# Where the weight tiles and the activations of a two-block transformer kernel begin in SBUF

## The chip, the cores and the metric

The kernel runs on one core of a Trainium2 chip. The metric is the device time in microseconds (us) of one launch. Tensors in SBUF are given here by the byte at which they begin within a partition; what this text calls the residue of a tensor is that byte modulo 512.

## What is computed

Two transformer blocks with 256 tokens and a model width of 1024, all in float32. The first block has two layers with a second stream of 256 context tokens; the second has one layer. Cut to what matters here:

```python
def swiglu(h, w_gu, w_down):
    gu = h @ w_gu
    return (jax.nn.silu(gu[..., :D_FF]) * gu[..., D_FF:]) @ w_down
...
    for i in range(DEPTH):            # first block, streams x and z (context)
        x = ffn_sublayer(x, mx, 0, g[0], g[1], ffn_w_gu[i, 0], ffn_w_down[i, 0])
        if ctx_needed:
            z = ffn_sublayer(z, mz, 0, g[0], g[1], ffn_w_gu[i, 0], ffn_w_down[i, 0])
        ...                           # window attention (i = 1) or short convolution (i = 0)
        x = ffn_sublayer(x, mx, 6, g[4], g[5], ffn_w_gu[i, 1], ffn_w_down[i, 1])
...
    for i in range(DEPTH_2):          # second block: two sparse attentions, gates, one swiglu
        proj = rms_norm(x, g_mix[i]) @ w_in[i]
        ...
        x = x + merged @ w_out[i]
        gate, up = jnp.split(rms_norm(x, g_ffn[i]) @ w_ffn_in[i], 2, axis=-1)
        x = x + (jax.nn.silu(gate) * up) @ w_ffn_out[i]
        ple_gate = jax.nn.sigmoid(rms_norm(x, g_ple[i]) @ w_ple_gate[i])
        x = x + ple_gate * (p[i] @ w_ple_proj[i])
```

## The kernel before

The weights stream through SBUF in units of up to 128 x 2048 float32 (1 MB), one after another in a fixed list, `UNITS`. A unit belongs to a phase such as `gu0b` (gate and up weights, second part, of feed-forward 0) or `dn0bx` (down weights, stream x). Each unit has two buffers of each of three kinds, taken by the unit's parity: the SyncE queue loads `w_raw`, ScalarE rounds it into `w_hi` (float32r, L1539), VectorE writes the remainder `w_raw - w_hi` into `w_lo` (L944). The activations are split in the same way into a high and a low tensor: `h0`/`h1` and `hid0`/`hid1` in the first block, `b2_h0`/`b2_h1`, `b2_h3_0`/`b2_h3_1` and `b2_hid0`/`b2_hid1` in the second. A product is then the sum of three float32r matmuls (`PARTS`): high weights with high activations, high with low, low with high. `feature_unit` (L560) issues them: for each 128 x 128 weight tile `k`, the weights are the stationary operand and 256 or 512 columns of the activations the moving one. Every matmul has its own weight load; PEld is TensorE's weight load in the profile. `gu3` moves 258 columns. `token_unit` (L574) has the roles exchanged: weights move, activations stand.

Two streams of 256 tokens lie beside each other in `h` and `hid`. Phases whose inputs are ready for both streams move 512 columns (`gu0a`, `dn0a`, `gu0b`, the same of feed-forwards 1 and 2, and `conv_b`); all others move 256. In the trace the tensors `b2_h` and `b2_h3` are both called `b_h`, `b2_hid` is called `b_hid`.

The tensors of SBUF lie one behind another in the order in which `build` allocates them, so each size moves all that follow. Some residues come from tensors that are only there to fill, such as `skip2`. Worked out from the order and the sizes:

| operand of TensorE | residue before | residue after |
|---|---|---|
| `w_hi`, `w_lo`, phases with 512 columns but `conv_b` | 192 | 192 |
| `w_hi`, `w_lo`, all other phases and `conv_b` | 192 | 0 |
| `h0`, `h1`, `b2_h`, `b2_h3` | 256 | 192 |
| `hid0`, `hid1` | 288 | 192 |
| `b2_hid`, `p_r` | 384 | 192 |
| `x`, `gate_tmp`, `prod`, `sq`, `ssum` | 192 | 128 |
| `y` | 0 | 448 |
| `mats` (identity, mean, swaps) | 192 | 192 |

All weight tiles within a unit are 512 or 1024 bytes apart, and the activation tiles 1024 or 2048, so the residue is the same for each matmul of a phase.

What orders the work around this: TensorE waits in `feature_unit` for `lo_made` (the half unit is split) and for `evac` of the unit two before. ScalarE's queue is written out by hand: behind the evacuation of unit u comes the second half of unit u+2 (`high_half(u + 2, 1)`) and then the first half of unit u+3 (`high_ahead`). The first half may begin when TensorE has done the first half of the unit that had the buffer before (`half_done`); the second half waits for `unit_done`. Where a unit is larger than the one before in its buffer (`grows`) the first half waits for `unit_done` too.

Of the kernel before, what the change touches and what calls it, by code (L numbers as in the profile page):

```python
# [134 lines left out]

def halves_by(tile, *names):

    return max(HALVED[u] + 1 for u in phase_units(*[n for n in names if n in FIRST]) if UNITS[u].ul == tile)


def grows(u):

    return UNITS[u].elems > UNITS[u - 2].elems or UNITS[u - 2].phase == "ple_proj"

# [9 lines left out]
def build(nc, t, out, vec_at):  # L154
# [3 lines left out]
    def sb(name, shape, dt=F32, stack=None):  # L158
        return (stack or mem).enter_context(nc.sbuf_tensor(name, list(shape), dt))
# [11 lines left out]
    w_hi = [sb(f"w_hi{j}", [P, UNIT], F32R) for j in range(2)]  # L171
    w_lo = [sb(f"w_lo{j}", [P, UNIT], F32R) for j in range(2)]
# [30 lines left out]
    apart.close()  # L203
    hid1 = [sb(f"hid{j}", [P, HID, T2], F32R, b1) for j in range(2)]
# [7 lines left out]
    sb("skip2", [P, 2, S], F32, b2)  # L212
# [4 lines left out]
    causal = sb("causal", [P, S + 30], F32, b2)  # L217
    p_r = [sb(f"p_r{j}", [P, 2, S], F32R, b2) for j in range(2)]
# [11 lines left out]
    hid2 = [sb(f"b2_hid{j}", [P, HID, S], F32R, b2) for j in range(2)]  # L230

# [270 lines left out]
    def tensor_program():  # L502
# [41 lines left out]
        def feature_unit(u, acts, kc, mt, ready=None, beside=None, one_bank=False):  # L544
            w = [w_[u % 2][:, 0:kc * mt * P].rearrange("p (k n) -> p k n", k=kc) for w_ in (w_hi, w_lo)]
# [19 lines left out]
        def token_unit(u, acts, beside=None):  # L565
            w = [w_[u % 2][:].rearrange("p (k n) -> p k n", k=NC) for w_ in (w_hi, w_lo)]
# [286 lines left out]
        def up_phase():  # L853
            for u in phase_units("w_up"):
                w = [w_[u % 2][:].rearrange("p (k n) -> p k n", k=NC) for w_ in (w_hi, w_lo)]
# [14 lines left out]
        def ple():  # L870
            u = FIRST["ple_proj"]
            w = [w_[u % 2][:].rearrange("p (k n) -> p k n", k=2) for w_ in (w_hi, w_lo)]
# [33 lines left out]
    def vector_program():  # L906
# [32 lines left out]
        def low_half(u, n):  # L939
            if u < len(UNITS):  # L940
                half = UNITS[u].elems // 2
                cols = slice(n * half, (n + 1) * half)
                dve.wait_ge(hi_made, 2 * u + n + 1)
                dve.tensor_tensor(w_lo[u % 2][:, cols], w_raw[u % 2][:, cols], w_hi[u % 2][:, cols].bitcast(F32),  # L944
                                  ALU.subtract).then_inc(lo_made, 1)
# [584 lines left out]
    def scalar_program():  # L1530
        def high_half(u, n):
            if u < len(UNITS):
# [4 lines left out]
                if u >= 2:  # L1537
                    act.wait_ge(half_done if n == 0 and not grows(u) else unit_done, u - 1)
                act.activation(w_hi[u % 2][:, cols], w_raw[u % 2][:, cols], ACT.Copy).then_inc(hi_made, 1)  # L1539
# [679 lines left out]
```

## Time and profile before

| | |
|---|---|
| median of 3 runs | 2189.11 us (2188.25 to 2189.54) |
| time of the profiled execution | 2193.29 us |
| span of the profiled execution | 2191.9 us |
| TensorE busy | 2117.4 us, 97% |
| VectorE busy | 1532.0 us, 70% |
| ScalarE busy | 1046.2 us, 48% |
| HBM read | 375.45 MB, 172 GB/s over the span |
| mean granted TensorE clock | 0.991 |

The profiled execution is 4.18 us longer than the median. The duration of a matmul in the profile is from its start to its modelled end and overlaps with the next one; what a stream of matmuls costs is the pitch, the time from one start to the next. Where a stretch is filled with matmuls of one kind, the pitch is (length of the stretch + duration of one) / (number of matmuls that touch it), since the number counts those in flight at both ends. A windows row gives the stretch and its length, then for each engine (PE, PEld, and where all are shown DVE, ACT, POOL) the busy time and in brackets the number of instructions, then the granted clock as a share of 2.4 GHz, the DMA share and the rate in GB/s.

### The profile page before, as it was taken

Reading aid. Unit: us, or ns where it says so; the run is one execution under the profiler, and the core shown is the slowest. Engines: PE = TensorE matmul, PEld = TensorE weight load, DVE = VectorE, ACT = ScalarE, POOL = GpSimd, SP = SyncE. Lnnn points to the kernel's source line nnn. Section 1 sums busy time; section 2 is a strip of 40 time slices with the busy share of each in tenths; the row PEclk is TensorE's granted clock in tenths of the full one; section 3 lists DMA queues with packets and bytes.
Section 4 is the critical chain, followed back from the end, with each engine's and each line's share of the span. In section 5 each row is a group of like instructions: output and inputs, shape, how many; then the busy total and the mean of one; then the engine's idle time right before and its main releaser. Section 6 shows DMA issues by size and latency. Waiting matters only on the chain. (4 is left out here: it accounts for less than half of the span.)

```text
span 2191.9 us, 35166 instructions
## 1 busy us (share of the span) xinstructions
PE 2117.4 (97%) x14546; PEld 1914.2 (87%) x14546; DVE 1532.0 (70%) x2435; ACT 1046.2 (48%) x1675; POOL 91.6 (4%) x67
## 2 busy tenths in 40 slices
PE   6999999999999999999999999998999799999998
PEld 4988889998899888899988899868999787799998
DVE  3665777887785667787566777876665677777665
ACT  5622224763584232367323236675444445655444
POOL 1000000100100000010000001001000001000000
PEclk9999999999999999999999999999999899999999
DMA  7545555555445455555555555403555541245554
GB/s 308 200 162 203 190 182 182 173 177 191 171 173 184 169 202 191 173 184 184 174 181 195 192 173 177 166 7 129 171 196 187 202 147 67 81 175 171 202 178 143
DMA packets 70014, 378.76 MB, mean 173 GB/s; under 512 B 7392, under 2 KB 12384, under 8 KB 42976
## 3 DMA queue, kind: packets, MB, share of 16 engines
q1 hardware_dynamic: 66960, 369.92, 48.0%
q10 hardware_dynamic: 2896, 6.60, 0.8%
q8 instruction: 115, 1.88, 0.3%
q14 instruction: 43, 0.35, 0.0%
HBM read 375.45 MB, written 1.05 MB: 172 GB/s over the span
## 5 line engine op out<-in xcount | busy, mean ns | idle before, releaser
L560 PE MATMUL ps_g<-h,w_hi 128*128 128x256 f32 (+2 forms) x4288 | 983.6, 324 | 14.0 <-DVE h L1049 8.0
L944 DVE TENSOR_TENSOR w_lo<-w_raw,w_hi 128x1024 fp32r<-128x1024 f32 (+2 forms) x614 | 690.7, 1128 | 337.6 <-ACT w_hi L1539 336.0
L1539 ACT ACTIVATE w_hi<-w_raw 128x1024 fp32r<-128x1024 f32 (+2 forms) x614 | 591.2, 968 | 548.0 <-PE ps_g L560 381.9
L560 PEld LDWEIGHTS ps_g<-h,w_hi 128*128 128x128 f32 x4288 | 716.0, 189 | 82.6 <-issue 15.8
L560 PE MATMUL ps_g<-h,w_lo 128*128 128x256 f32 (+2 forms) x2144 | 688.9, 321 | 0.0
L560 PE MATMUL ps_g<-hid,w_hi 128*128 128x256 f32 (+1 forms) x2368 | 494.8, 306 | 1.9 <-DVE hid L1247 0.9
L560 PEld LDWEIGHTS ps_g<-h,w_lo 128*128 128x128 f32 x2144 | 404.8, 189 | 33.7
L560 PEld LDWEIGHTS ps_g<-hid,w_hi 128*128 128x128 f32 x2368 | 383.5, 189 | 25.8 <-DVE w_lo L944 1.4
L560 PE MATMUL ps_g<-hid,w_lo 128*128 128x256 f32 (+1 forms) x1184 | 361.2, 305 | 0.0
L560 PE MATMUL ps_g<-b_h,w_hi 128*128 128x256 f32 x1504 | 276.5, 285 | 10.2 <-DVE b_h L1049 7.2
L560 PEld LDWEIGHTS ps_g<-b_h,w_hi 128*128 128x128 f32 x1504 | 232.1, 190 | 18.0 <-issue 16.9
L560 PEld LDWEIGHTS ps_g<-hid,w_lo 128*128 128x128 f32 x1184 | 222.2, 188 | 11.0
L560 PE MATMUL ps_g<-b_h,w_lo 128*128 128x256 f32 x752 | 211.4, 281 | 0.0
L909 DVE CUSTOM_DVE_ANT_0 ps_s<-mod_raw,cond_b,vecs 128x1024 f32<-128x1024 f32 x128 | 164.9, 1288 | 15.6 <-DMA mod_raw<-in_w_mod 15.6
L909 DVE CUSTOM_DVE_ANT_0 mod_raw<-mod_raw,cond_b,vecs 128x1024 f32<-128x1024 f32 x128 | 169.3, 1322 | 0.0
L1686 ACT ACTIVATE gate_tmp<-ps_g 128x256 f32<-128x256 f32 (+1 forms) x102 | 48.7, 478 | 247.0 <-PE ps_g L560 246.9
L2004 POOL TENSOR_TENSOR ssum<-ssum,sq 128x512 f32<-128x512 f32 x56 | 81.0, 1446 | 1972.4 <-ACT sq L1564 1972.4
L1098 DVE TENSOR_TENSOR prod<-gate_tmp,ps_g 128x512 f32<-128x512 f32 (+1 forms) x86 | 48.3, 562 | 135.1 <-ACT gate_tmp L1686 135.1
L560 PEld LDWEIGHTS ps_g<-b_h,w_lo 128*128 128x128 f32 x752 | 142.7, 190 | 0.0
L560 PE MATMUL ps_g<-b_hid,w_hi 128*128 128x256 f32 x352 | 60.4, 277 | 2.8 <-DVE w_lo L944 1.4
L1139 DVE TENSOR_TENSOR hid<-prod,hid 128x256 fp32r<-128x256 f32 (+1 forms) x108 | 57.5, 532 | 0.0
L1737 ACT ACTIVATE hid<-prod 128x256 fp32r<-128x256 f32 (+1 forms) x108 | 54.0, 500 | 6.2 <-DVE prod L1098 5.1
(274 smaller groups left out, 1592.8 us busy)
## 6 DMA issues: line engine op xcount, KB each, us to landing
w_raw<-in_gu SPq DMA_DIRECT2D x130, 1024.0 KB, 4.8
mod_raw<-in_w_mod SPq DMA_DIRECT2D x128, 512.0 KB, 3.5
w_raw<-in_conv_cu SPq DMA_DIRECT2D x16, 1024.0 KB, 4.8
w_raw<-in_dn00b SPq DMA_DIRECT2D x16, 768.0 KB, 4.2
w_raw<-in_dn01b SPq DMA_DIRECT2D x16, 768.0 KB, 4.2
w_raw<-in_dn10b SPq DMA_DIRECT2D x16, 768.0 KB, 4.2
w_raw<-in_conv_out SPq DMA_DIRECT2D x8, 1024.0 KB, 4.8
w_raw<-in_w_in_a SPq DMA_DIRECT2D x8, 1024.0 KB, 5.4
```

The source lines that it names most:

```text
L560: mm = pe.matmul(at, w[wp][:, k, m * P:(m + 1) * P], acts[ap][:, k, cs], start=(k == 0 and n == 0 and not (one_bank and m)), stop=(k == kc ...
L909: return dve.tensor_tensor_reduce(into, w, cond_b[:, s, :], 1.0, b_mod[:, g, s:s + 1], ALU.mult, ALU.add, mod_sb[:, g, s:s + 1])
L944: dve.tensor_tensor(w_lo[u % 2][:, cols], w_raw[u % 2][:, cols], w_hi[u % 2][:, cols].bitcast(F32), ALU.subtract).then_inc(lo_made, 1)
L1098: dve.tensor_tensor(prod[:, j, cs], gate_tmp[:, j, cs], ps_g[:, 2 * j + 1, cs], ALU.mult).then_inc(evac, 1)
L1139: dve.tensor_tensor(hid[1][:, ul, cs], prod[:, j, cs], hid[0][:, ul, cs].bitcast(F32), ALU.subtract).then_inc(half_lo, 1)
L1539: act.activation(w_hi[u % 2][:, cols], w_raw[u % 2][:, cols], ACT.Copy).then_inc(hi_made, 1)
L1686: act.activation(gate_tmp[:, j, cs], ps_g[:, 2 * j, cs], ACT.Silu if ph[:2] == "gu" else ACT.Copy).then_inc(gate_made, 1)
L1737: act.activation(hid[0][:, ul, cs], prod[:, j, cs], ACT.Copy).then_inc(half_hi, 1)
L2004: pool.tensor_tensor(ssum[:, s, :], ssum[:, s, :], sq[:, s, :], ALU.add).then_inc(sq_added[s], 1)
```

## The change

Weight tiles get two places in their buffers. Phases that move 512 columns (except `conv_b`) have them at one place, all others 80 elements (320 bytes) further, modulo 128 elements. The two starts of each buffer (`HI_STARTS`, `LO_STARTS`) make up for where the buffer itself lies, so that high and low tiles of both parities have one residue. The buffers are longer by 80 or 96 elements, and `fill0`, `fill1` and `fill2` (with `skip2` taken away) put `h`, `hid`, `b2_h`, `b2_hid` and `p_r` all at residue 192. The operands of ScalarE's and VectorE's split and of all of TensorE's units follow. No instruction is added, removed or moved in order, and no shape changes.

Where a unit begins further up in a buffer than the unit before it did, ScalarE's write of its first half would run into weights that TensorE has yet to read; there the wait is for `unit_done` instead of `half_done` (`moves_up`). By the list of units that holds for 12 of them: the first two units of `gu0a`, `dn0bx`, `gu1a`, `dn1bx`, `gu2a` and `dn2bx`.

```diff
+def weight_slot(u):
+    return 0 if UNITS[u].cols == BOTH and UNITS[u].phase != "conv_b" else 80
+
+HI_STARTS, LO_STARTS = (0, 80), (48, 0)
+
+def weight_at(u, starts):
+    return (weight_slot(u) - starts[u % 2]) % P
...
+def moves_up(u):
+    return any(weight_at(u, starts) > weight_at(u - 2, starts) for starts in (HI_STARTS, LO_STARTS))
...
-    w_hi = [sb(f"w_hi{j}", [P, UNIT], F32R) for j in range(2)]
-    w_lo = [sb(f"w_lo{j}", [P, UNIT], F32R) for j in range(2)]
+    w_hi = [sb(f"w_hi{j}", [P, UNIT + (80, 96)[j]], F32R) for j in range(2)]
+    w_lo = [sb(f"w_lo{j}", [P, UNIT + 80], F32R) for j in range(2)]
+    sb("fill0", [P, 32])
...
+    sb("fill1", [P, 120], F32, b1)
     hid1 = [sb(f"hid{j}", [P, HID, T2], F32R, b1) for j in range(2)]
...
-    sb("skip2", [P, 2, S], F32, b2)
...
+    sb("fill2", [P, 96], F32, b2)
     p_r = [sb(f"p_r{j}", [P, 2, S], F32R, b2) for j in range(2)]
...
+    def hi_of(u):
+        at = weight_at(u, HI_STARTS)
+        return w_hi[u % 2][:, at:at + UNIT]
...
-            w = [w_[u % 2][:, 0:kc * mt * P].rearrange("p (k n) -> p k n", k=kc) for w_ in (w_hi, w_lo)]
+            w = [w_[:, 0:kc * mt * P].rearrange("p (k n) -> p k n", k=kc) for w_ in (hi_of(u), lo_of(u))]
...
-                dve.tensor_tensor(w_lo[u % 2][:, cols], w_raw[u % 2][:, cols], w_hi[u % 2][:, cols].bitcast(F32),
+                dve.tensor_tensor(lo_of(u)[:, cols], w_raw[u % 2][:, cols], hi_of(u)[:, cols].bitcast(F32),
...
-                    act.wait_ge(half_done if n == 0 and not grows(u) else unit_done, u - 1)
-                act.activation(w_hi[u % 2][:, cols], w_raw[u % 2][:, cols], ACT.Copy).then_inc(hi_made, 1)
+                    act.wait_ge(unit_done if n or grows(u) or moves_up(u) else half_done, u - 1)
+                act.activation(hi_of(u)[:, cols], w_raw[u % 2][:, cols], ACT.Copy).then_inc(hi_made, 1)
```

## Rows read from the trace of the kernel before

**Rows 1.** The page: busy time of each engine, and TensorE's granted clock in slices
```profile
PE 2117.4 (97%) x14546; PEld 1914.2 (87%) x14546; DVE 1532.0 (70%) x2435; ACT 1046.2 (48%) x1675; POOL 91.6 (4%) x67
...
PEclk9999999999999999999999999999999899999999
```

**Rows 2.** Lines by form: L560's groups, count, busy us, mean ns, idle before
```profile
L560 PE MATMUL ps_g<-h,w_hi 128*128 128x512 f32 x1600 | 498.4, 393 | 0.0
L560 PE MATMUL ps_g<-h,w_hi 128*128 128x256 f32 x1984 | 357.9, 282 | 5.9 <-DVE h L1041 2.9 <-DVE prod L1098 1.5 <-DVE w_lo L944 1.3
L560 PE MATMUL ps_g<-hid,w_hi 128*128 128x256 f32 x1888 | 343.5, 283 | 1.9 <-DVE hid L1247 0.9 <-DVE y L1116 0.8
...
L560 PE MATMUL ps_g<-b_h,w_hi 128*128 128x256 f32 x1504 | 276.5, 285 | 10.2 <-DVE b_h L1049 7.2 <-DVE qk L1346 2.6 <-DVE b_h L1442 0.4
...
L560 PE MATMUL ps_g<-hid,w_hi 128*128 128x512 f32 x480 | 151.3, 396 | 0.0
L560 PE MATMUL ps_g<-h,w_hi 128*128 128x258 f32 x704 | 127.5, 284 | 8.0 <-DVE h L1049 8.0
...
L560 PE MATMUL ps_g<-b_hid,w_hi 128*128 128x256 f32 x352 | 60.4, 277 | 2.8 <-DVE w_lo L944 1.4 <-DVE x L1116 1.4
```

**Rows 3.** Windows of L560: stretch, length, PE busy (count), PEld busy (count), clock, DMA, GB/s
```profile
470.00:510.00 40.00, 40.00 (x342) 40.00 (x341) 1.00 0.57 194
344.00:374.00 30.00, 30.00 (x253) 30.00 (x252) 1.00 0.66 228
1600.00:1666.00 66.00, 66.00 (x559) 66.00 (x558) 1.00 0.52 185
2055.00:2120.00 65.00, 65.00 (x554) 65.00 (x553) 1.00 0.55 189
2027.00:2052.00 25.00, 25.00 (x223) 25.00 (x223) 1.00 0.63 209
215.00:340.00 125.00, 125.00 (x548) 102.57 (x547) 1.00 0.54 187
157.00:208.00 51.00, 51.00 (x220) 41.05 (x219) 1.00 0.50 180
```

**Rows 4.** Timeline of w_up (L865): start us, busy us, instruction, count
```profile
1920.99 0.39 PE L865 MATMUL ps_g<-b_hid,w_hi 128*128 128x256 f32 x2
...
1921.34 0.39 PE L865 MATMUL ps_g<-b_hid,w_hi 128*128 128x256 f32 x2
...
1921.67 0.39 PE L865 MATMUL ps_g<-b_hid,w_hi 128*128 128x256 f32 x2
```

**Rows 5.** Windows of L865: w_up while the clock is 1.2 GHz, and after
```profile
1922.20:1925.20 3.00, 3.00 (x16) 3.00 (x15) 0.50 0.84 289
...
1928.00:1944.00 16.00, 16.00 (x138) 16.00 (x137) 1.00 0.43 138
```

**Rows 6.** Line L574, two token units: duration ns min/median/max, first and last start
```profile
L574 PE MATMUL ps_g<-w_hi,b_h x32: 281/281/384, 1796.2 to 1801.7; 128*128 128x256 f32 x32
...
L574 PE MATMUL ps_g<-w_hi,b_h x32: 276/276/366, 1805.4 to 1810.7; 128*128 128x256 f32 x32
```

**Rows 7.** Windows, all engines: conv_cux, conv_outx, w_in_d, dn4b
```profile
416.00:466.00 50.00, 49.28 (x403) 48.72 (x404) 42.52 (x57) 36.28 (x62) 3.44 (x2) 1.00 0.48 169
555.00:578.50 23.50, 23.42 (x196) 23.21 (x195) 21.93 (x27) 12.61 (x16) 3.20 (x2) 1.00 0.51 184
1817.00:1918.00 101.00, 98.06 (x777) 75.69 (x776) 75.76 (x299) 58.21 (x184) 5.54 (x4) 0.98 0.21 75
2120.70:2157.20 36.50, 33.66 (x290) 32.92 (x288) 22.08 (x32) 17.21 (x26) 2.94 (x2) 1.00 0.46 154
```

**Rows 8.** The chain of waits within dn4b: start us, us, what
```profile
2122.58 0.97 DVE w_lo L944
...
2123.57 4.18 DMA w_raw<-in_dn2b
...
2141.69 1.62 DVE w_lo L944
```

**Rows 9.** Timeline of ScalarE where gu0b (512 columns) gives way to dn0bx (256)
```profile
341.31 0.60 ACT L1686 ACTIVATE gate_tmp<-ps_g 128x512 f32<-128x512 f32 x1 [4.59 <-PE ps_g L560]
341.81 0.84 ACT L1539 ACTIVATE w_hi<-w_raw 128x768 fp32r<-128x768 f32 x1
```

More of the change, by code:

```diff
@@ L230, in build, with lo_of @@
     hid2 = [sb(f"b2_hid{j}", [P, HID, S], F32R, b2) for j in range(2)]
+    def hi_of(u):
+        at = weight_at(u, HI_STARTS)
+        return w_hi[u % 2][:, at:at + UNIT]
+    def lo_of(u):
+        at = weight_at(u, LO_STARTS)
+        return w_lo[u % 2][:, at:at + UNIT]
     b_mod = vecs[:, vec_at["b_mod"]:vec_at["b_mod"] + 2 * N_MODS].rearrange("p (m s) -> p m s", s=2)
@@ L565, in token_unit @@
         def token_unit(u, acts, beside=None):
-            w = [w_[u % 2][:].rearrange("p (k n) -> p k n", k=NC) for w_ in (w_hi, w_lo)]
+            w = [w_.rearrange("p (k n) -> p k n", k=NC) for w_ in (hi_of(u), lo_of(u))]
             pe.wait_ge(lo_made, 2 * u + 2)
@@ L854, in up_phase @@
             for u in phase_units("w_up"):
-                w = [w_[u % 2][:].rearrange("p (k n) -> p k n", k=NC) for w_ in (w_hi, w_lo)]
+                w = [w_.rearrange("p (k n) -> p k n", k=NC) for w_ in (hi_of(u), lo_of(u))]
                 for src in range(2):
@@ L871, in ple @@
             u = FIRST["ple_proj"]
-            w = [w_[u % 2][:].rearrange("p (k n) -> p k n", k=2) for w_ in (w_hi, w_lo)]
+            w = [w_.rearrange("p (k n) -> p k n", k=2) for w_ in (hi_of(u), lo_of(u))]
             pe.wait_ge(p_lo, 1)
```

## The prediction, made before the changed kernel ran

> **What bounds the kernel now.** I read the page first: TensorE is busy 97% of the span, the next engine 70%, and the clock is full in nearly every slice [rows 1]. So TensorE's stream sets the time. Then the lines by form, for what the stream consists of: nearly all of it is L560 in a few forms [rows 2]. The counts there are those with `w_hi`; by `PARTS` each form has half as many again with `w_lo`. With 256 columns that makes 2976 matmuls on `h`, 2832 on `hid`, 2256 on `b_h`, 528 on `b_hid`; 1056 on `h` with 258 columns; with 512 columns 2400 on `h` and 720 on `hid`. The idle time before them is 29 us in these rows, little against 2190.
>
> Then windows that lie inside one phase and are filled with L560, since the pitch is what counts [rows 3]. Pitch = (length + duration of one) / count, with durations of 0.28 us (0.39 at 512 columns) from [rows 2]:
> - conv_cuz (470 to 510), `h`, 256 columns: 40.28/342 = 117.8 ns
> - dn0bx (344 to 374), `hid`: 30.28/253 = 119.7
> - gu3b (1600 to 1666), `h`, 258 columns: 66.28/559 = 118.6
> - gu4b (2055 to 2120), `b_h`: 65.28/554 = 117.8
> - dn4a (2027 to 2052), `b_hid`: 25.28/223 = 113.4
> - gu0b (215 to 340), `h`, 512 columns: 125.39/548 = 228.8
> - dn0a (157 to 208), `hid`, 512 columns: 51.39/220 = 233.6
>
> The reader should see that one shape, 128x256, has three pitches, and they go with the residue of the moving tensor: with weights at 192, activations at 256 give 117.8, at 288 give 119.7, at 384 give 113.4. DVE and ACT do nothing to these stretches, PE is busy in all of each. At 512 columns 288 is again slower than 256, by 4.8 ns. PEld is busy all the time at 256 columns and 80% at 512: the load of the next weights always runs beside a moving stream. The distance from activation to weight residue is thus a cost, and the change sets it: to 192 bytes (192 minus 0, as dn4's 384 minus 192) in phases of 256, to 0 in those of 512.
>
> **Against this speaks the Trainium skill.** "TensorE: Matmul & The Clock Gate", Part 2, says that TensorE has two independent SBUF read ports and that loading the next tile's weights takes nothing from the running matmul. By that rule the placement changes nothing; it is a rival below. The rows of dn4a and gu4b contradict it, by 4.4 ns a matmul in one shape [rows 3]. The same page's gap formula, N/2.4 + 2.5 ns, would put an undisturbed matmul at an estimated 109 ns for 256 columns and 216 for 512.
>
> **Term 1, 256 columns.** dn4a is the one row with the new distance, so 113.4 is what I take. `h`: 2976 x (117.8 - 113.4) = 13.1 us. `b_h`: 2256 x 4.4 = 9.9. 258 columns: 113.4 x 258/256 = 114.3, 1056 x 4.3 = 4.5. `hid`: 2832 x 6.3 = 17.8. `b_hid`: nothing. Together 45.3; the mean clock of 0.991 means about 2% of the span at 1.2 GHz, where [rows 5] show 3.41/16 = 213 ns, which is 256 columns at 1.2 GHz with nothing on top, so nothing to save: 44.5 us. That residues count as a distance and not each by itself is an assumption: no row has weights at 0.
>
> **Term 2, the long pitch.** One distance can have two pitches. w_up has dn4's residues. It runs three matmuls in 0.33 to 0.35 us, 113 ns each, before the clock drops [rows 4], and after the clock is back 16.28/138 = 118.0, to its end [rows 5]. Two token units with the same operands' residues (weights now moving) show 281 ns of duration in one and 276 in the next [rows 6]; 276 is dn4's. So the stream can lock into a long pitch of 118 or a short one of 113, and a drop of the clock or a pause may decide which. dn4 itself went into the short one. I take a quarter of the 9120 matmuls to be caught: 2280 x 4.4 = 10 us lost. The ends are 0 and all of them.
>
> **Term 3, 512 columns, distance 0.** No row has it. At distance 96 the pitch is 233.6, at 64 it is 228.8; a line through the two gives 219.2 at 0. The other end is 228.8, no further gain. I take 222, nearer to the line, since the same step from 96 to 64 also helps at 256 columns. `conv_b` (192 of the 2400) gets distance 192 with 512 columns, which no row shows, and is left at 228.8, plus or minus 1 us. Sum: 2208 x 6.8 + 720 x 11.6 = 15.0 + 8.4 = 23.4 us; ends 3.5 (only `hid` gains) and 2208 x 9.6 + 720 x 14.4 = 31.6.
>
> **Term 4, what doesn't reach the end.** A faster stream shortens the cover of other engines. VectorE is busy 85% in conv_cux and 93% in conv_outx, 75% in w_in_d with two attentions' chains [rows 7]: of the 960 matmuls there, 4 us of saving may be lost. Down phases have the shortest units: at 113 ns a unit of 36 takes 4.1 us, and a load of its weights takes 4.18 from issue to landing, with a split behind it [rows 8]. dn4b runs at that pitch and has 33.66 us of work in 36.50 [rows 7], so up to 2.8 us is lost in each of seven such phases that now run at 119.7, if their saving of 1.8 each allows; I take 3 us over all.
>
> The new wait (`moves_up`) delays ScalarE's first half for 12 units. Behind it in ScalarE's queue stands the evacuation of the unit that TensorE has just finished, whose VectorE product and `hid` tile dn0bx needs. In [rows 9] that evacuation comes at 341.31, at once when the unit is done; the first half, 0.85 us long by the row behind it, now stands ahead of it. dn0bx needs the last `hid` tile only after 33 of its matmuls, 3.7 us, and that hides most: 0 to 0.8 us at three places, I take 1. Before gu0a the next unit is 11 us off (48 x 228.8 ns), which hides it all. The fp32 matmuls (mean, transposes) get other distances too; no row prices them, and I take 0 within plus or minus 1.5 us. Term 4: 8 us.
>
> **Sum.** 44.5 + 23.4 - 10 - 8 = 49.9 us off 2193.3, the profiled execution's time: 2143.4. The median of the runs is 4.2 below that: 2139.
>
> **The rivals.**
> 1. The long pitch holds at 256 columns almost everywhere. For it: w_up stays at it for the rest of its phase, and few places reset the stream, since residues no longer change between w_up and the end. Against it: dn4 was entered from a 117.8 stream. `hid` gains 2832 x 1.9 = 5.4, dn4 loses 528 x 4.4 = 2.3, 512 columns give 23.4, less 4 for cover: 22 us, 2167.
> 2. As 1, and distance 0 does nothing at 512 columns: 5.4 - 2.3 + 3.5 = 7 us, 2183.
> 3. Nothing moves, by the skill's rule of independent ports, or because the residues count each by itself and weights at 0 are no better than `h` at 256: 2189, with 512 columns unchanged.
> 4. Slower: at distance 0 both streams start in the same place of SBUF and collide on every matmul. The trend from 96 to 64 speaks against it, but 0 lies outside the two rows. `hid` already shows what a worse distance does, 4.8 ns. If 512 columns take 238, that is 2208 x 9.2 + 720 x 4.4 = 23.5 us more; with rival 1's 3.1 of gain the kernel is 20 us slower, 2209. It decides from 231 ns at 512 columns, if the long pitch holds too; with term 1 whole it would need 243.
>
> **How the numbers follow.** Forecast 2139 with chance 0.65 (its own range 2117 to 2162: terms 1 and 3 whole with term 4 halved give 44.5 + 31.6 - 4 = 72 off, and half the matmuls at the long pitch with term 3 at 10 give some 27); rival 1 0.20; rival 2 0.05; rival 3 0.05; rival 4 0.05. The range 2110 to 2173 leaves out the last three and the edges. About 0.2% is what a measurement of this kernel can tell from no change. Faster: 0.65 + 0.20 + 0.05 = 0.90; same 0.05; slower 0.05.
>
> **What would show it.** In windows of the same phases: 113.4 at `h`, `hid` and `b_h` (duration 276) shows term 1, 118 with 281 the long pitch; gu0b and dn0a at one pitch near 222 shows term 3, one at or above 229 refutes it; both should be equal, since they have one distance. `conv_b` apart from gu0a shows whether 0 was needed. Gaps in front of dn0bx's last tiles and in conv_outx price term 4. I am wrong if a phase with weights at 0 and activations at 192 differs from dn4a before, without a drop of the clock ahead of it.

## The result, and the profile after

| | before | after |
|---|---|---|
| median | 2189.11 us | 2177.78 us |
| lowest to highest, 7 runs each | 2183.54 to 2190.56 | 2172.7 to 2182.31 |
| profiled execution, its span | 2193.29, 2191.9 | 2176.27, 2174.7 |

The ratio is 0.9947, with a 95% interval of 0.9935 to 0.9959. The change makes the kernel 0.5% faster, where 2.3% was forecast, and the time lies above the forecast's range of 2110 to 2173.

In this text a distance is the residue of the weight tiles minus that of the activations, modulo 512. Before, the distances were 448 (`h`, `b_h`), 416 (`hid`) and 320 (`b_hid`). After the change there are two: 0 in phases with 512 columns, 320 in all others and in `conv_b`. The prediction counted from the other side, so its 64, 96 and 192 are 448, 416 and 320 here.

The page of after, busy time by engine and the granted clock; the answer to [rows 1]:

```profile
PE 2091.3 (96%) x14546; PEld 1892.2 (87%) x14546; DVE 1529.4 (70%) x2435; ACT 1043.1 (48%) x1675; POOL 90.8 (4%) x67
...
PEclk9999999999999999999999999999999999999999
```

TensorE's busy share fell from 97% to 96%: besides a faster stream there is more idle time. The lines by form, with mean duration and idle time before the group, answer [rows 2] (L560 is now L588, L944 is L972, L1116 is L1144, L1539 is L1567):

```profile
L588 PE MATMUL ps_g<-h,w_hi 128*128 128x512 f32 x1600 | 493.2, 390 | 0.0
L588 PE MATMUL ps_g<-h,w_hi 128*128 128x256 f32 x1984 | 353.1, 282 | 7.5 <-DVE h L1069 3.8 <-DVE prod L1126 2.2 <-DVE w_lo L972 1.1
L588 PE MATMUL ps_g<-hid,w_hi 128*128 128x256 f32 x1888 | 331.6, 280 | 7.1 <-DVE y L1144 4.5 <-DVE hid L1275 0.9 <-DVE w_lo L972 0.6
...
L588 PE MATMUL ps_g<-h,w_hi 128*128 128x258 f32 x704 | 130.2, 287 | 7.5 <-DVE h L1077 7.5
```

Two things stand out. The form with 258 columns got slower, 284 to 287 ns. And before `hid` there is a wait for `y`, VectorE's addition of a finished down unit to the result, of 4.5 us, which was 0.8.

Windows of TensorE inside single phases answer [rows 3]. In order: conv_cuz, gu1az, dn0bx, gu3b, gu4b, dn4a, dn3a, gu0b, dn0a, conv_b. Columns: stretch, length, busy (count), clock, DMA share, GB/s:

```profile
468.00:508.00 40.00, 40.00 (x342) 1.00 0.56 197
660.00:690.00 30.00, 30.00 (x257) 1.00 0.56 199
344.00:373.00 29.00, 28.57 (x241) 1.00 0.63 224
1600.00:1656.00 56.00, 56.00 (x465) 1.00 0.52 179
2042.00:2102.00 60.00, 60.00 (x532) 1.00 0.55 195
2014.00:2038.00 24.00, 24.00 (x214) 1.00 0.64 223
1565.00:1588.00 23.00, 23.00 (x197) 1.00 0.65 227
222.00:336.00 114.00, 114.00 (x505) 1.00 0.54 187
158.00:206.00 48.00, 48.00 (x214) 1.00 0.52 188
512.00:552.00 40.00, 40.00 (x173) 1.00 0.56 197
```

Taken as before, (length + duration) / count, with 0.28 and 0.39 us: conv_cuz 117.8, gu1az 117.8, dn3a 118.2, but gu4b 113.3 and dn4a 113.5, all with 256 columns at one distance. gu3b is at 121.0, which was 118.6. gu0b is at 226.5 and dn0a at 226.1 (one matmul more or less in the count is 1 ns there), conv_b at 233.5. dn0bx has gaps.

From the starts of all matmuls in the two traces, each pitch added up by kind, and what goes beyond a pitch counted as a pause:

| part | before, us | after, us | change | mean pitch, ns |
|---|---|---|---|---|
| 256 columns, `h` | 350.5 | 346.4 | -4.1 | 117.8 to 116.4 |
| 256 columns, `b_h` (both) | 268.4 | 260.9 | -7.5 | 117.8 to 114.5 |
| 256 columns, `hid` | 339.6 | 326.1 | -13.5 | 119.9 to 115.2 |
| 256 columns, `b_hid` | 82.5 | 81.8 | -0.7 | 114.6 to 113.6 |
| 258 columns | 125.4 | 127.6 | +2.2 | 118.7 to 120.8 |
| 512 columns, `h` with `conv_b` | 549.4 | 545.4 | -4.0 | 228.9 to 227.2 |
| 512 columns, `hid` | 168.0 | 163.2 | -4.8 | 233.3 to 226.7 |
| fp32 matmuls (mean, transposes) | 166.9 | 168.9 | +2.0 | 131.0 to 132.6 |
| pauses in float32r phases | 50.3 | 65.1 | +14.8 | |
| extra cost of the stretches at 1.2 GHz | 12.3 | 11.0 | -1.3 | |

That adds up to 16.9 of the 17.2 us by which the span is shorter. The streams gained 32 us and the pauses took half of it back.

The fp32 row isn't a price of their new distances. At full clock the median pitch of every form of them is the same in both traces (216.0 ns for the 256-column mean matmuls), and all of them together differ by 0.4 us. 1.1 of the 2.0 us come from five more mean matmuls that ran at 1.2 GHz in the second trace, at 427 ns each.

**Where the pauses are.** The waits of TensorE after the change (waiting line, what it waited for: us, times, longest):

```profile
PE ps_s L560 <- POOL ssum L2032: 20.8, 5, 12.9
...
PE ps_g L588 <- DVE y L1144: 4.5, 10, 0.9
```

and of before:

```profile
PE ps_s L532 <- POOL ssum L2004: 18.1, 4, 13.3
...
PE ps_g L560 <- DVE y L1116: 0.8, 3, 0.3
```

Of the 14.8 us by which the pauses grew, 10.7 lie in six phases, the second down projections of feed-forwards 0 to 2, `dn0bx` to `dn2bz`: 6.1 us of pauses before, 16.8 after. (A pause taken from the starts is some 0.16 us longer than the idle time that the profile gives, since a matmul's duration reaches that far beyond its pitch.) By what released TensorE there, the waits for `y` grew from 1.3 to 6.4 us, those for GpSimd's sum `ssum`, a part of the norm that follows `y`, from 1.1 to 3.7, and those for the last `hid` tile from nothing to 1.0. Added up, the six phases last 220.1 us before and 222.7 after, although their 1728 matmuls take 5.2 ns less each on average. The reason can be read from VectorE's queue in dn1bz. Timeline of the additions to `y` there (start us, busy us), before:

```profile
960.51 0.41 DVE L1116 TENSOR_TENSOR y<-y,ps_g 128x256 f32<-128x256 f32 x1
...
965.09 0.42 DVE L1116 TENSOR_TENSOR y<-y,ps_g 128x256 f32<-128x256 f32 x1
...
969.15 0.41 DVE L1116 TENSOR_TENSOR y<-y,ps_g 128x256 f32<-128x256 f32 x1
...
977.11 0.41 DVE L1116 TENSOR_TENSOR y<-y,ps_g 128x256 f32<-128x256 f32 x1
```

and after:

```profile
956.92 0.41 DVE L1144 TENSOR_TENSOR y<-y,ps_g 128x256 f32<-128x256 f32 x1
...
961.50 0.42 DVE L1144 TENSOR_TENSOR y<-y,ps_g 128x256 f32<-128x256 f32 x1
...
965.55 0.41 DVE L1144 TENSOR_TENSOR y<-y,ps_g 128x256 f32<-128x256 f32 x1
...
973.49 0.42 DVE L1144 TENSOR_TENSOR y<-y,ps_g 128x256 f32<-128x256 f32 x1
```

The steps are 4.58, 4.06 and 7.96 us before, and 4.58, 4.05 and 7.94 after. VectorE keeps its own beat there, while a unit of 36 matmuls went from 4.32 to 4.08 us (at 113.3 ns). Between the additions its queue holds the splits (L972, 0.95 us each) and the norm of the first stream (a reciprocal of 1.76 us and pieces of 0.68), and it waits for ScalarE's splits in between. A matmul stream that is faster than that beat only waits.

### The profile page after: what moved, and what is told of

The parts are those of the page before. It is cut to its first block and busy times, and to the rows that moved or that the text cites. A ratio compares the mean times of both kernels' runs of the same rounds, so it can differ in the third digit from the quotient of the medians.

```text
span 2174.7 us, 35166 instructions
## 1 busy us (share of the span) xinstructions
PE 2091.3 (96%) x14546; PEld 1892.2 (87%) x14546; DVE 1529.4 (70%) x2435; ACT 1043.1 (48%) x1675; POOL 90.8 (4%) x67
## 5 line engine op out<-in xcount | busy, mean ns | idle before, releaser
L588 PE MATMUL ps_g<-h,w_hi 128*128 128x256 f32 (+2 forms) x4288 | 976.4, 323 | 15.0 <-DVE h L1077 7.5
L972 DVE TENSOR_TENSOR w_lo<-w_raw,w_hi 128x1024 fp32r<-128x1024 f32 (+2 forms) x614 | 691.4, 1129 | 349.1 <-ACT w_hi L1567 347.8
L1567 ACT ACTIVATE w_hi<-w_raw 128x1024 fp32r<-128x1024 f32 (+2 forms) x614 | 590.4, 968 | 564.6 <-PE ps_g L588 385.0
L588 PEld LDWEIGHTS ps_g<-h,w_hi 128*128 128x128 f32 x4288 | 716.0, 189 | 82.2 <-issue 15.3
L588 PE MATMUL ps_g<-h,w_lo 128*128 128x256 f32 (+2 forms) x2144 | 690.4, 322 | 0.0
L588 PE MATMUL ps_g<-hid,w_hi 128*128 128x256 f32 (+1 forms) x2368 | 479.4, 302 | 7.1 <-DVE y L1144 4.5
L588 PEld LDWEIGHTS ps_g<-h,w_lo 128*128 128x128 f32 x2144 | 406.8, 190 | 31.6
L588 PEld LDWEIGHTS ps_g<-hid,w_hi 128*128 128x128 f32 x2368 | 377.0, 188 | 30.8 <-issue 4.4
L588 PE MATMUL ps_g<-hid,w_lo 128*128 128x256 f32 (+1 forms) x1184 | 355.7, 300 | 0.0
L588 PE MATMUL ps_g<-b_h,w_hi 128*128 128x256 f32 x1504 | 269.9, 283 | 10.5 <-DVE b_h L1077 7.4
L588 PEld LDWEIGHTS ps_g<-b_h,w_hi 128*128 128x128 f32 x1504 | 230.6, 191 | 18.5 <-issue 17.1
L588 PEld LDWEIGHTS ps_g<-hid,w_lo 128*128 128x128 f32 x1184 | 223.2, 189 | 9.4
L588 PE MATMUL ps_g<-b_h,w_lo 128*128 128x256 f32 x752 | 210.3, 280 | 0.0
L588 PEld LDWEIGHTS ps_g<-b_h,w_lo 128*128 128x128 f32 x752 | 143.6, 191 | 0.0
L588 PE MATMUL ps_g<-b_hid,w_hi 128*128 128x256 f32 x352 | 60.4, 277 | 3.2 <-DVE w_lo L972 1.6
```

The source lines that it names most:

```text
L588: mm = pe.matmul(at, w[wp][:, k, m * P:(m + 1) * P], acts[ap][:, k, cs], start=(k == 0 and n == 0 and not (one_bank and m)), stop=(k == kc ...
L972: dve.tensor_tensor(lo_of(u)[:, cols], w_raw[u % 2][:, cols], hi_of(u)[:, cols].bitcast(F32), ALU.subtract).then_inc(lo_made, 1)
L1567: act.activation(hi_of(u)[:, cols], w_raw[u % 2][:, cols], ACT.Copy).then_inc(hi_made, 1)
```

## The experiments

Each was run beside the kernel before on the same chip. Pitches of single units are medians of the distance between starts in the trace. "Short" is 113.3 ns and "long" 117.8 ns for 256 columns; their durations in the profile are 276 and 281 ns.

**1. The same kernel once more** (after_again, no edit).

> The changed kernel once more, for a second trace. Distance here and below is (weight residue - activation residue) mod 512, in bytes: 448 for h and 416 for hid before, 320 for dn4 before, 0 and 320 in the changed kernel. Theory A: at distance 320 and 256 columns the stream of TensorE has two pitches, 113.3 and 117.8 ns, and keeps the one it has until a pause; pauses differ by nanoseconds between executions, so the phases that run long change from trace to trace (gu0az, conv_cuz, gu1az, dn3a and dn3b ran long, gu2az, gu4a and gu4b short). Some of these eight flip, and the span moves by up to 10 us. Rival B: the long pitch belongs to the place in the program; then the same phases are long and the span is within 2 us of 2174.7. Both expect 226.7 ns at 512 columns.

2179.01 us. gu1az, then gu4b and dn4a, in windows like those above:

```profile
655.00:687.00 32.00, 32.00 (x284) 1.00 0.57 198
```

```profile
2042.00:2102.00 60.00, 60.00 (x511) 1.00 0.55 194
2014.00:2038.00 24.00, 24.00 (x206) 1.00 0.68 225
```

32.28/284 = 113.7: gu1az went from long to short, and by the unit medians dn3a and dn3b did too. gu4b went from 113.3 to 60.28/511 = 118.0 and dn4a from 113.5 to 24.28/206 = 117.9, and gu2az and most of gu4a went to long too. conv_cuz and gu0az were long again. The program and all places are identical. So at distance 320 the pitch is one of two states; it holds through whole phases, and which one comes up differs between executions. Of all 256-column matmuls whose duration is one of the two, 40% were long in after and 54% here.

**2. All distances, upward and downward** (sweep_up, sweep_down). Each unit of the phases that are free for it gets its own distance, in steps of 16 bytes, in one kernel rising and in the other falling:

```diff
-    return 0 if UNITS[u].cols == BOTH and UNITS[u].phase != "conv_b" else 80
+    step = 16                                    # -16 in sweep_down
+    give("gu0b", [step * n for n in range(12)])
+    give("gu1b", [step * (12 + n) for n in range(12)])
...
+    give("gu4a", [step * n for n in range(10)])
+    give("gu4b", [step * (10 + n) for n in range(12)])
...
```

> Each unit of the undisturbed phases gets a distance of its own, in steps of 16 bytes, rising from unit to unit (512 columns: gu0b, gu1b, gu2b and dn0a to dn2a; 258: gu3a and gu3b; 256: gu4a, gu4b, conv_cuz, gu1az, gu2az, dn3, dn4). The activations begin where they did before the change. Theory A: the pitch is a function of the distance, smooth but for one or two steps, the same for h, b_h and hid; at 512 columns 229 at 448, 233.5 at 416, 226.7 at 0, 233.4 at 320; at 256 columns 117.8 at 448, 120 at 416, 113.3 or 117.8 at 320. The best distance at 512 columns gives 226 or less; that at 256 columns 113 or less. Rival C: the start of each tensor counts by itself; then the units don't reproduce these values, since weights now begin elsewhere.

> As sweep_up with the distances falling from unit to unit, so that each distance is met by another unit, after another neighbour and in other phases. Theory A: the same pitch at each distance within 0.5 ns wherever it has one value, and two values only around 320 with 256 columns, by what the stream did before (hysteresis). Rival D: the pitch depends on the unit's phase or place; then the two sweeps disagree by more than 1 ns at many distances.

2201.9 and 2197.26 us. Windows of sweep_up: gu0b at distances 0 and 16, then at 32, 48 and 64; gu4b at 192, at 224, at 240:

```profile
211.00:231.00 20.00, 20.00 (x90) 1.00 0.55 203
232.00:264.00 32.00, 32.00 (x139) 1.00 0.54 191
2073.30:2078.50 5.20, 5.20 (x49) 1.00 0.59 205
2084.40:2089.60 5.20, 5.20 (x47) 1.00 0.58 202
2090.20:2095.40 5.20, 5.20 (x45) 1.00 0.62 205
```

20.39/90 = 226.6 and 32.39/139 = 233.0; the three short windows run at 112 to 122 and show the order only, the unit medians are 113.3, 116.7 and 120.0. The medians of both kernels together, which repeat with a period of 256 bytes:

| distance modulo 256 | 512 columns | 256 columns |
|---|---|---|
| 0 | 226.7 to 227.5 | 119.5 to 120.0 |
| 16 | 226.7, three of eight times 233.4 | 118.2 to 118.5 |
| 32 | 233.3 | 118.3 |
| 48 | 233.3 | 117.8 to 118.3, once 123.3 |
| 64 (the 320 of the change) | 233.3 | 113.3 or 117.8 |
| 80 | 231.9 | 118.7 to 119.0 |
| 96 | 234.3 | 117.3 to 120.0 |
| 112 to 160 (`hid` before: 160) | 232.3 to 233.5 | 118.3 to 120.2, at 144 twice 116.7 |
| 176 | 229.8 to 230.2 | 118.1 |
| 192 (`h` before) | 228.8 to 229.0 | 113.3 or 117.8 |
| 208, 224 | 231.8 to 233.4 | 116.5 to 116.7 |
| 240 | 226.7, once 228.3 | 118.5 to 120.0 |

`h` and `hid` at one distance have one pitch, so the pitch goes by the distance and not by the start of either tensor. The rest of what I expected did not come: the curve isn't smooth, no distance is below 226 or 113, and two values at one distance are found not only at 64 but also at 192, 16 (512 columns), 96 and 144. The lowest pitches are 226.7 at 512 columns and 113.3 at 256, half of it. They are reached at different distances, and where 512 columns are best, 256 are among the worst. With 258 columns most distances give 120 to 122, 64 and 320 give 120.7 to 120.9, and the lower values came in one direction each: 118.8 at 192 rising (122.2 falling), 119.0 at 448 falling, 116.7 at 240 (120.0 rising) and 117.7 at 496, both falling. The 240 and 496 were not taken up in any later kernel. At 320 or 64 a unit that came from 16 bytes below was short five times of five, from 16 above twice of four.

**3. Everything 64 bytes further** (shift64).

```diff
+    sb("fill3", [P, 16])
```

> The changed kernel with 64 bytes more ahead of w_raw: weights at residues 256 and 64, activations at 256, all distances between them as in the changed kernel. Theory A (only the distance counts): 226.7 ns in gu0b and dn0a, 233.4 in conv_b, 113.3 or 117.8 with 256 columns, span 2165 to 2185. Rival C (each start counts by itself): gu0b at another pitch, by 2 ns or more.

2168.98 us, 35% long. gu1b, conv_b and gu3b, in windows:

```profile
785.00:900.00 115.00, 115.00 (x509) 1.00 0.54 184
512.00:548.00 36.00, 36.00 (x156) 1.00 0.55 199
1600.00:1650.00 50.00, 50.00 (x416) 1.00 0.53 189
```

115.39/509 = 226.7, 36.39/156 = 233.3, 50.28/416 = 120.9: all as in after. Residues count as a distance; the prediction had assumed that. The lower time goes with fewer long phases, and is a single run.

**4. Distance 320 everywhere** (all_320).

```diff
-    return 0 if UNITS[u].cols == BOTH and UNITS[u].phase != "conv_b" else 80
+    return 80
```

> The changed kernel with the weights at distance 320 in all phases, those of 512 columns included, so that no unit moves up and no first half waits longer for it. From the two sweeps: 233.3 ns instead of 226.7 in the 2928 matmuls of 512 columns outside conv_b, 19.4 us more; the pauses in front of dn0bx, dn1bx and dn2bx's last tiles (0.33 us each in the changed kernel) vanish, 1 us less. Expected 2178 + 18 = 2196 us, ratio to the kernel before 1.003. Rival: if the moved waits cost more than that (0.5 us and more at each of the 6 handovers), the time is 2190 or less.

2191.79 us, ratio 1.0009 (0.9995 to 1.0023). gu0b, same stretch as above:

```profile
222.00:336.00 114.00, 114.00 (x491) 1.00 0.53 182
```

114.39/491 = 233.0. The 512-column streams take 19.4 us more than in after (560.0 and 168.0 us). So the split into two slots is needed; with the one slot at 320 the change would have been worth nothing. The time is 4 us below the 2196 that I expected; the profiled executions, 17.1 us apart, agree with the streams. No unit moves up here, so none has the added wait, and the six down phases still pause for 15.0 us and last 221.1. The wait is worth some 1.6 us at most: in after, TensorE pauses 0.33 us for the last `hid` tile, behind the 33rd matmul of dn0bx, dn1bx and dn2bx, and here it doesn't.

**5. Half of distance 320 undone: 448 where 256 or 258 columns move** (hold_448). 512 columns stay at 0, `conv_b` is at 448 too.

```diff
-    return 0 if UNITS[u].cols == BOTH and UNITS[u].phase != "conv_b" else 80
+    return 0 if unit.cols == BOTH and unit.phase != "conv_b" else 448
```

> All phases that move 256 or 258 columns, and conv_b, get distance 448, which is h's distance in the kernel before; 512 columns stay at distance 0. Nothing is left out. Theory 1 (distance 448 is always long, as every phase on h was in the kernel before): h and b_h at 117.8, hid at 117.8 instead of 119.9, gu3 118.7, conv_b 229; 256 columns cost as before less 5 us on hid, 512 columns save 11 to 13 us, pauses about 6 us over before: median 2178 to 2182. Theory 2 (448 has both pitches, as units in the two sweeps show, and what comes before decides): some phases at 113.3, spread as at 320; then 15 to 25 us below theory 1's streams and a median near 2172 to 2176.

2184.17 us, ratio 0.9978 (0.9965 to 0.9992). gu4b and gu1b:

```profile
2048.00:2108.00 60.00, 60.00 (x512) 1.00 0.53 185
...
785.00:905.00 120.00, 120.00 (x531) 1.00 0.56 190
```

60.28/512 = 117.7 and 120.39/531 = 226.7. Theory 1 held for the pitches, with few exceptions: 96% of the 256-column matmuls whose pitch is one of the two were long, and the short ones were single units. In the sweeps, units at 448 entered from 464 or 432 were short in 2 cases of 5. So 448 can be short, but is nearly never entered that way. The time is 2 us above what I expected. It isn't for the pauses, which rose by 6.3 us in all, as expected: 512 columns gained 9.6 us instead of 11 to 13, and `b_hid`, which goes from 113.4 to 117.8 here, lost 2.3 that I had left out. Of the pauses, 13.9 us are in the six down phases. Their matmuls went from 120.0 only to 117.4 ns, 4.5 us less in all, and the six still lasted 224.1 us, 4 us more than before. The moved wait accounts for 1.6 us of it by all_320; what the rest comes from is not shown. A stream faster by 2.6 ns was already of no use there.

Against hold_448, the change puts 256 columns (and 258, and `conv_b`) at 320. By the two ratios, 0.9978 and 0.9947, about 5 us of the change's 11.6 come from distance 0 at 512 columns and `hid` off 416, and about 7 from distance 320; the two ratios come from different sets of runs.

**6. Which half of the loop paces the down phases** (thin_loads, thin_splits).

```diff
+THIN = ("dn0bx", "dn0bz", "dn1bx", "dn1bz", "dn2bx", "dn2bz")
...
+            n = 64 if unit.phase in THIN else unit.elems                 # thin_loads
...
+                cols = slice(n * half, n * half + 64 if UNITS[u].phase in THIN else (n + 1) * half)   # thin_splits
```

> The changed kernel with the weight loads of dn0bx, dn0bz, dn1bx, dn1bz, dn2bx and dn2bz cut to 64 of 1280 or 1536 columns; the splits then work on what is in the buffers, so part of the computation is left out. These six phases have 17 us of pauses of TensorE in the changed kernel and 6 us in the kernel before. Theory E: a unit of 36 matmuls at 113 ns is over sooner than its successor's weights are loaded and split, and the load is the longest part; the pauses fall to 6 us or less and the span by 8 to 11 us. Rival F: VectorE's order of work (split, product, mod product) makes the pauses; then they stay within 3 us of 17.

> The changed kernel with VectorE's low split in the same six phases cut to 64 columns a half, the loads whole; part of the computation is left out. VectorE gets 0.9 us a half back, 85 us in all. Theory E (the load is the longest part): the pauses stay above 10 us. Rival F (VectorE's queue): they fall from 17 us to 6 or less.

| | pauses in the six phases | their length | time |
|---|---|---|---|
| before | 6.1 | 220.1 | 2193.29 |
| after | 16.8 | 222.7 | 2176.27 |
| thin_loads | 8.8 | 213.0 | 2168.46 |
| thin_splits | 2.3 | 210.6 | 2160.8 |

The phase dn1bz in after, then in thin_splits (stretch, length, then busy time and count of PE, PEld, DVE, ACT, POOL):

```profile
943.20:982.80 39.60, 37.15 (x301) 35.74 (x300) 30.39 (x41) 28.32 (x47) 6.65 (x5) 1.00 0.49 170
```

```profile
938.70:974.60 35.90, 35.90 (x303) 35.58 (x301) 19.96 (x39) 27.41 (x45) 6.44 (x5) 1.00 0.52 176
```

Both kernels leave out part of the computation, and each is a single run. With 10 us less of splits on VectorE, TensorE is busy through the whole phase and it is 3.7 us shorter. That refutes the theory that the load alone sets the pace, which wanted 10 us of pauses to stay. Shorter loads help too: they take 8.0 of the 16.8 us of pauses away where the thinner splits take 14.5, and the six phases get 9.7 and 12.1 us shorter. That refutes the other theory, VectorE's queue alone. So it is a loop of load, ScalarE's split and VectorE's split. VectorE is idle for 9 of the 39.6 us in after: it is late, not full.

**7. High and low tiles apart** (sweep_parts). 49 units get every pair of distances from 272 to 368 for `w_hi` and `w_lo`.

```diff
+    pairs = [(a, c) for a in OFFSETS for c in OFFSETS]
+    return {u: (320 + a, 320 + c) for u, (a, c) in zip(free, pairs)}
```

> The high and the low weights get distances of their own, in all 49 pairs of -48 to +48 bytes around 320, one pair to each of 49 undisturbed units with 256 columns, activations at residue 256. The question is whether a pair has a pitch that is short by itself. Theory A (what counts is the distance of each load to the stream beside it): the mean of a unit lies between the values of its two distances in the sweeps (117.8 at 304, 113.3 or 117.8 at 320, 118.7 at 336, 118.3 at 288), and a pair that pulls the stream back into the short lock gives 113 to 115 every time. Rival: no pair gives less than 116.5 but (320, 320).

2192.95 us. All pairs ran at 117.3 to 121.6 ns, but (352, 368) at 115.5, one unit; equal distances of 320 at 117.8. No pair ran at 113.3. It doesn't tell how one gets into the short state, and found no pair of unequal places that does it.

**8. One unit at another distance to push the stream into the short state** (kick_304, kick_304b, kick_336, kick_none). From the sweeps: one unit at 304 ahead of the phase, so that 320 is entered from below. kick_336 is the same from above, kick_none has the same buffers and no such unit. In kick_304 each such unit also makes a later unit move up in its buffer, so that eight more first halves wait for `unit_done`.

```diff
+KICKS = (("gu0ax", 3), ("conv_cux", 5), ("gu1ax", 5), ("gu2ax", 5), ("dn3a", 0), ("dn3b", 0), ("gu4a", 1),
+         ("w_in_a", 1))                          # () in kick_none
...
+    if (unit.phase, unit.ul) in KICKS:
+        return 304                               # 336 in kick_336
```

> The changed kernel, all tensors 224 bytes further, with eight units at distance 304 instead of 320: gu0ax 3, conv_cux 5, gu1ax 5, gu2ax 5, dn3a 0, dn3b 0, gu4a 1, w_in_a 1, each behind the last pause of a stretch of 256 columns. In the sweeps the stream was short (113.3) in 5 of 5 units that came at 320 or 64 from 16 bytes below (304 or 48), while at 304 it always ran 117.8. Theory H (hysteresis: the distance met last sets the lock, and it holds to the next pause): every unit behind such a unit is short up to the next pause, about 83 units in all, where about half were long in the changed kernel: 6 to 9 us less than without these units. Rival J (chance at each change of distance): about half of them are short, no gain.

> The same kernel as kick_304 for a second trace. Theory H: the same units short as there. Rival J: other units.

> As kick_304 with 336 in the eight units. From 16 bytes above, 320 or 64 was short in 2 of 4 units of the sweeps. Theory H: some of the eight stretches long, some short, and the span between that of kick_304 and 9 us more.

> The layout of kick_304 without the eight units: the changed kernel 224 bytes further. Theory A (only distances count): 226.7 at 512 columns, 233.4 in conv_b, about half of the undisturbed stretches of 256 columns long, time within 5 us of the changed kernel's 2178. Rival C (each start counts): another pitch at 512 columns.

kick_304: 2178.19 us, ratio 0.9957 (0.9945 to 0.9969); kick_none: 2176.36 us, ratio 0.9944 (0.9925 to 0.9963); kick_304b 2176.29 and kick_336 2177.8. Counted by the unit right behind it, the stream was short 12 times of 16 behind the unit at 304, in the two executions, and 3 of 8 behind the one at 336. But in kick_none, without any such unit, the same eight places were short 7 of 8 times, and 19 of 24 with the two kernels of experiments 9 and 10, which have none either. So it is not shown that the push does anything, and the 5 of 5 of the sweeps may have been chance. Theory H fell also by kick_304b, where other units were short than in kick_304. Nothing is seen in the time: 52% long in kick_304, 36% in kick_304b, 41% in kick_none. Where does the state change? gu4a, then dn4a of kick_304:

```profile
1958.00:2010.00 52.00, 51.88 (x451) 1.00 0.53 180
2014.00:2038.00 24.00, 24.00 (x207) 1.00 0.57 194
```

Short in gu4a behind its kick unit (its unit medians are 113.3), then 24.28/207 = 117.3 over dn4a. The change is not at the phase's border, where the moving tensor changes and the distance does not. Windows of dn4a's first 3 us and of the 3 us behind its first 28 matmuls:

```profile
2014.90:2017.90 3.00, 3.00 (x29) 1.00 0.09 31
2018.10:2021.10 3.00, 3.00 (x28) 1.00 0.73 224
```

3.28/29 = 113.1, then 3.28/28 = 117.1. In the starts, 27 pitches of dn4a are of 113 and 114 ns, the next is 122 ns, and from there on it is long. The 28th matmul, whose pitch that is, is one that waits for semaphores, the last `hid` tile's among them. The same happens at the same matmul in kick_none and kick_304b, with 122 and 123 ns. In ten traces (after, and all of experiments 1, 3, 4, 8, 9 and 10) each other change of state lies behind a pause, a change of distance, or a change from moving weights to moving activations. So the part of my theory by which only a delay or a change of distance resets the state stands, but it can be a delay as small as 8 ns. Which state comes next stays open: in after, the same matmul has 119 ns, in best 121, and both streams stayed short. The loads set in there too (DMA share 0.09, then 0.73); in after it goes from 0.08 to 0.66, and the stream stays short.

**9. What the sweeps suggest** (best). As kick_none, with 258 columns at 448 and `conv_b` at 0.

```diff
     if unit.phase[:3] == "gu3":
-        return 320
-    return 0 if unit.cols == BOTH and unit.phase != "conv_b" else 320
+        return 448
+    return 0 if unit.cols == BOTH else 320
```

> As kick_none (distance 320 at 256 columns, 0 at 512), but gu3 (258 columns) at 448 and conv_b at 0. Nothing is left out. If each phase's pitch goes by its own distance: gu3 120.8 to 118.7, 1056 x 2.1 = 2.2 us, and conv_b 233.4 to 226.7, 192 x 6.7 = 1.3 us, so 3 us below kick_none, 2173. If the share of long and short phases, which no distance sets, outweighs this: anything from 2168 to 2180, with gu3 and conv_b at their new pitches all the same.

2174.59 us (2165.65 to 2178.84, 4 runs), ratio 0.9923 (0.9893 to 0.9952). conv_b and gu3:

```profile
505.00:547.00 42.00, 42.00 (x187) 1.00 0.56 198
```

```profile
1594.00:1650.00 56.00, 56.00 (x474) 1.00 0.53 182
```

42.39/187 = 226.7, against 233.4: 1.3 us over the 192 matmuls. 56.28/474 = 118.7, against 120.8: 2.2 us over 1056. Both pitches came out as expected. The medians of best and of kick_none, 1.8 us apart, have overlapping ranges, so that the gain in time is likely but not shown. The profiled execution of best, 2165.65 us, is its fastest, with 29% long, the fewest of all.

**10. VectorE's other work in the down phases** (best_mods). Two of three modulation products move out of each of dn0bx, dn1bx and dn2bx, both into the last unit of gu0b, gu1b and gu2b ahead of it.

```diff
-                      ("dn0bx", 1, slice(0, 6, 2)), ("conv_b", 2, slice(None)), ("conv_outx", 1, slice(0, 2)),
+                      ("dn0bx", 1, slice(0, 2, 2)), ("conv_b", 2, slice(None)), ("conv_outx", 1, slice(0, 2)),
```

> As best, with part of the modulation products taken off dn0bx, dn1bx and dn2bx (one of three left in each) and one more in gu0b, gu1b and gu2b, so that VectorE has less to do in those down phases. Nothing is left out. If VectorE's load there makes TensorE's pauses, they fall from 3.7 us in the three phases to about 1.5 and the kernel gains 1 to 3 us on best. If the loop of load, ScalarE and VectorE alone makes them, they stay within 0.5 us and so does the time, apart from phases that go long or short.

2173.32 us (2171.06 to 2175.59, 4 runs), ratio 0.9922 (0.9902 to 0.9942). The pauses in dn0bx, dn1bx and dn2bx rose from 3.9 to 6.3 us, against what I expected; those in the `z` phases behind them fell from 12.4 to 8.0. The rise is one new wait for `y` of some 1.6 us in each, right behind the first down unit: in dn0bx VectorE works on the two moved products from 341.55 to 346.46 us and reaches the addition to `y` only at 347.24. The six phases last 219.9 us instead of 222.5. So VectorE's products in the `x` phases delay what the `z` phases wait for, the norm among it, and moving them only moved a part of the waiting. Against best the time is the same within both ranges.

## Why the prediction was wrong, point by point

The forecast, 2139, was 38.8 us below the measured 2177.78. That pitch goes by distance was right. Two steps failed: term 3, whose pitch at distance 0 was drawn from a line through two points, and the bound, by which every faster matmul shortens the kernel. Term 2's share was too small besides.

**The bound.** "TensorE's stream sets the time" holds in most phases, and fails in six, 220 us long. The 97% busy in [rows 1] hid it: there the two paces were nearly equal before, and TensorE's pauses were 6 us. The prediction took 6.3 ns off each of the 1728 matmuls there, 10.9 us; measured, these phases got 2.6 us longer. I looked for tight places where units are shortest (dn4b) [rows 7, 8] and in the conv phases, and did take "up to 2.8 us" for each of seven down phases as lost, but then only 3 us over all. In conv_cux, conv_outx and w_in_d, for which I took 4 us, the pauses grew by 0.2 us together.

**Term 1, 256 columns,** 45.3 us. That dn4a's distance can have dn4a's pitch is right: 113.3 ns in every phase that is short. `hid` gained more than any (13.5). 258 columns was mis-sized in sign: I took 4.5 us of gain by scaling 256 columns, and it cost 2.2 us. Distance 320 is bad for 258 columns, though they differ by two; a row of its own was needed.

**Term 2, the long pitch,** 10 us. The mechanism was right, and read from [rows 4 to 6]; the share was not. 40% of the matmuls were long in after and 54% in after_again, not 25%. Measured against 113.4, `h`, `b_h`, `hid` and `b_hid` gained 25.8 us instead of 40.8 (the 45.3 without 258 columns): 15 us lost, or 3400 matmuls at 4.4 ns. The changes do lie at pauses and delays, as I had thought, but what decides which state follows is not shown. In the kernel before, `h` in `feature_unit` was always long [rows 3], and hold_448, 96% long, shows that this goes with its distance. My own sign of being wrong came true too: gu1az and conv_cuz have weights at 0 and activations at 192 and ran at 117.8, with no drop of the clock since the last stretch in the short state.

**Term 3, 512 columns at distance 0,** 23.4 us, is where most is missing: 8.8 us. I drew a line through two pitches to 219.2 and took 222. The measured floor is 226.7, at distances 0, 240 and (mostly) 16; at 32 it is 233.3 again. The curve has steps and a narrow dip, and no line through two of its points says where it ends. The lower end that I gave, 3.5 us, had `h` gain nothing. `conv_b` was left at 228.8 plus or minus 1; it went to 233.4, as the sweep and all_320 show for that distance.

**Term 4, what doesn't reach the end,** 8 us. Pauses grew by 14.8 us, 10.7 of it in the six down phases, and the fp32 matmuls by 2.0. That my 0 for the fp32 matmuls' new distances was right is seen from their unchanged pitches; 1.1 of the 2.0 come from where a 1.2 GHz stretch fell, and the rest I can't assign. The moved wait was right in place and size: TensorE pauses 0.33 us, three times, for the last `hid` tile behind 33 matmuls, 1.0 us where I took 1. all_320, which has none, has 1.8 us less of pauses in those phases.

By these differences: 6.7 (258 columns) + 5.0 (share of long) + 14.6 (512 columns) + 8.8 (term 4) = 35.1 us. Of this go 1.3 for the stretches at 1.2 GHz, which cost less than before, and the 0.8 that the prediction had taken off for them. The profiled execution was forecast at 2143.4 and came at 2176.27, 32.9 above.

**The rivals.** Rivals 1 (2167) and 2 (2183) lie on either side of the measured time, and neither with its mechanism: long was about half of the 256-column matmuls and not nearly all, and at 512 columns 8.8 of the 23.4 us came, neither all of it nor the 3.5 us of rival 2. Rival 4, a collision at distance 0, is refuted at 512 columns. At 256 columns distance 0 is indeed among the worst, with 120 ns, but other distances reach 120 too, and a collision is not shown. Rival 3 is refuted by all_320 against after: the same instructions and shapes, and 6.7 ns a matmul between two places at 512 columns. The Trainium skill's rule of two independent read ports ("TensorE: Matmul & The Clock Gate", Part 2), from which the prediction drew that placement changes nothing, does not hold as far as that for these streams, where every matmul has its own weight load: by the distance it is 226.7 to 234.3 ns at 512 columns and 113.3 to 120 at 256. Whether the ports are what costs, no run here shows. The same part's gap formula for a warm matmul by itself gives an estimated 216 and 109 ns in the Trainium skill; no placement reached them here.

## What to carry to other kernels

Where every matmul loads its own weights, where the two operands begin in SBUF was worth up to 6% of a matmul here (113.3 against 120 ns): measure the pitch at all distances in one kernel, a unit each, instead of drawing a line through two, and do it for each number of columns that moves. Before a faster stream is counted, compare the beat of the other engines in each phase: where the steps between VectorE's evacuations don't depend on TensorE, a faster matmul is worth nothing, even if TensorE hardly pauses there, as in these six phases before (6 of 220 us). And a pitch with two states should be counted by its shares over several executions, not by the state of one trace.

## What the hardware showed that I had not expected

- At one distance and one shape, 256 columns run at 113.3 or at 117.8 ns, for whole phases and in the same program: gu4b was short in one execution of after and long in the next. It changes at pauses and at changes of distance, and in three traces a delay of 8 or 9 ns at a waiting matmul was enough. What chooses the next state stays open: behind a unit at 304 the stream was short 12 of 16 times in experiment 8, behind one at 336 3 of 8, and without either 7 of 8 (kick_none).
- The pitch repeats over distances with a period of 256 bytes, not 512: 64 and 320, 192 and 448, 0 and 256 are alike in all forms measured, but for single units and the two values that some distances have.
- 258 columns, two more than 256, have another curve: at 448 they run at 118.7 where 256 run at 117.8, but at 320 at 120.8 where 256 reach 113.3. Their lowest was 116.7, in one unit at 240, where 256 columns give 118.5 to 120.0.
- The fastest pitch at 256 columns is exactly half of the fastest at 512 (113.3 and 226.7): what stands on top of the columns at 2.4 GHz, 6.7 and 13.3 ns, is no fixed number of ns for each matmul. At 1.2 GHz there is nothing on top for 256 columns [rows 5].
